# A diffusion trunk on one core: the first vectors in blocks, attention heads in pairs, the norm chain reordered, and unread matmuls in five norms' waits

## The reference

```python
def rmsnorm(x, g): return x * rsqrt(mean(x * x) + 1e-6) * g
def ffn_half(x, (shift, scale, gate), g, w_gu, w_d):
    hg, hu = split((rmsnorm(x, g) * (1 + scale) + shift) @ w_gu)      # D_FF = 2816
    return x + 0.5 * gate * ((silu(hg) * hu) @ w_d)
for l in range(2):
    xl, xc = ffn_half(xl, ...), ffn_half(xc, ...)
    hl, hc = modulated rmsnorm of each
    l == 0: conv = silu(layernorm(depthwise_conv31(val * sigmoid(gate))))
            att  = window attention, 8 heads of 64, 2 KV heads, rotary, a sink per head;
                   latents see latents within 128 and all the context, context sees context
            y = concat(conv, att) @ w_out
    l == 1: y = bidirectional chunkwise mLSTM, 4 heads of 256, output for the latents only
    x += gate * y; ffn_half again (layer 1: latents only)
return rmsnorm(xl, final_norm)
```

## Time and profile before

| | us |
|---|---|
| runs | 1919.63, 1926.95, 1926.68 (median 1926.68) |
| profiled execution | 1918.44, of which the span from first to last instruction 1916.7 |
| PE matmuls busy | 1819.4 (95%) |
| DVE / ACT busy | 869.5 (45%) / 626.4 (33%) |
| mean granted PE clock | 0.974 |

### The profile page before, as it was taken

One profiled execution on the slowest core, in us unless ns is written; L12 is line 12 of the kernel. 1 busy time (PEld: TensorE's weight loads), 2 busy tenths in 40 slices (PEclk: granted clock), 3 DMA queues, 4 the chain that ended last, 5 costly groups with the idle time before them and its releaser, 6 DMA issues.

```text
span 1916.7 us, 25184 instructions
## 1 busy us (share of the span) xinstructions
PE 1819.4 (95%) x10083; PEld 1490.1 (78%) x10083; DVE 869.5 (45%) x1335; ACT 626.4 (33%) x849; POOL 36.2 (2%) x72
## 2 busy tenths in 40 slices
PE   3999999999889999999999999999998999899996
PEld 1788888877544668888888688888886998889996
DVE  2433332345878663333233633333344436765554
ACT  2332122223445432222222432222224323544342
POOL 0000000000001000000000000000000000000000
PEclk7999999999899989999999999999998999999998
DMA  8522452243138444222323422233123212354543
GB/s 340 225 88 88 176 191 94 69 153 146 45 130 309 154 158 172 103 83 101 109 71 101 180 88 95 86 105 109 63 93 153 88 67 90 110 197 174 188 170 105
DMA packets 39107, 252.39 MB, mean 132 GB/s; under 512 B 4464, under 2 KB 5872, under 8 KB 14448
## 3 DMA queue, kind: packets, MB, share of 16 engines
q1 hardware_dynamic: 29232, 179.91, 26.5%
q0 software_dynamic: 9792, 71.31, 9.7%
HBM read 250.15 MB, written 1.05 MB: 131 GB/s over the span
## 4 chain that ended last, share of the span: by engine, by line
PE 90%; DVE 5%; ACT 2%; issue 1%; DMA 1%; SPq 0%; ACTq 0%; DVEq 0%
PE ps L432 27%; PE ps L434 27%; PE ps L433 27%; PE ps L468 3%; DVE w_lo L1176 1%; PE ps L632 1%; DMA xT<-in_xT 1%; DVE y L1359 1%; PE ps L606 1%; PE ps L745 1%; PE ps L774 1%; PE ps L492 1%; ACT w_hi L877 1%; PE ps L615 1%; DVE acc L1189 0%
## 5 line engine op out<-in xcount | busy, mean ns | idle before, releaser
L432 PE MATMUL ps<-hn_hi,w_hi 128*128 128x512 f32 (+2 forms) x1784 | 648.6, 364 | 10.2 <-DVE hn_lo L1253 8.3
L433 PE MATMUL ps<-hn_lo,w_hi 128*128 128x512 f32 (+2 forms) x1784 | 640.8, 359 | 0.0
L434 PE MATMUL ps<-hn_hi,w_lo 128*128 128x512 f32 (+2 forms) x1784 | 640.4, 359 | 0.0
L1176 DVE TENSOR_TENSOR w_lo<-raw,w_hi 128x2048 fp32r<-128x2048 f32 (+2 forms) x184 | 377.0, 2049 | 566.3 <-ACT w_hi L877 566.1
L877 ACT ACTIVATE w_hi<-raw 128x2048 fp32r<-128x2048 f32 (+2 forms) x184 | 316.6, 1721 | 777.5 <-PE ps L434 774.1
L432 PEld LDWEIGHTS ps<-hn_hi,w_hi 128*128 128x128 f32 (+1 forms) x1784 | 339.5, 190 | 74.8 <-issue 21.8
L434 PEld LDWEIGHTS ps<-hn_hi,w_lo 128*128 128x128 f32 (+1 forms) x1784 | 339.4, 190 | 50.5
L433 PEld LDWEIGHTS ps<-hn_lo,w_hi 128*128 128x128 f32 (+1 forms) x1784 | 339.8, 190 | 48.6 <-issue 0.5
L432 PE MATMUL ps<-a_hi,w_hi 128*128 128x512 f32 (+1 forms) x704 | 255.6, 363 | 1.7 <-DVE a_lo L1291 1.7
L433 PE MATMUL ps<-a_lo,w_hi 128*128 128x512 f32 (+1 forms) x704 | 255.2, 363 | 0.0
L434 PE MATMUL ps<-a_hi,w_lo 128*128 128x512 f32 (+1 forms) x704 | 255.2, 362 | 0.0
(11 more groups left out here) (189 smaller groups left out, 1162.4 us busy)
## 6 DMA issues: line engine op xcount, KB each, us to landing
raw<-in_w_up SPq DMA_DIRECT2D x88, 1024.0 KB, 4.8
mod_raw<-in_mod_w POOLq DMA_DIRECT2D x68, 1024.0 KB, 7.3
raw<-in_w_downA SPq DMA_DIRECT2D x32, 768.0 KB, 4.3
raw<-in_w_downB SPq DMA_DIRECT2D x32, 640.0 KB, 3.9
raw<-in_w_od_in SPq DMA_DIRECT2D x16, 1024.0 KB, 4.8
raw<-in_w_ev_in SPq DMA_DIRECT2D x7, 1024.0 KB, 4.8
mod_raw<-in_mod_w SPq DMA_DIRECT2D x4, 1024.0 KB, 10.1
raw<-in_w_ev_out SPq DMA_DIRECT2D x4, 1024.0 KB, 4.8
```

The lines of the kernel that those rows point to most:

```text
L432: pe.matmul(o, lh, rh, start=first, stop=False)
L433: pe.matmul(o, lh, rl, start=False, stop=False)
L434: return pe.matmul(o, ll, rh, start=False, stop=last)
L1176: dve.tensor_tensor(w_lo[:, u0 % 2, 0:n], raw[:, u0 % 2, 0:n], w_hi[:, u0 % 2, 0:n], ALU.subtract).then_inc(lo_made, 1)
```

## The change

- **Start.** x is loaded first, in four transfers. Jobs 0 and 1 are stored as eight blocks, one for each output tile k, with both vectors' columns; `block_products`, `block_columns`, `block_rows` and `block_vectors` make the two vectors of tile k just ahead of tile k's normalisation. POOL begins with job 2.
- **Norm chain.** The first square goes straight to acc and the last is not added: PE sums acc and sq[1] in two accumulating matmuls, so each norm has 6 additions instead of 8 and no clearing. The split of the second next unit (LATE_UNIT) moves from ahead of the last square and the reciprocal to behind the root on ACT and behind rstd on DVE.
- **Two units side by side.** `first_units` works the first two units after a norm tile by tile together for 5 tiles (2 tiles where there are 256 tokens), then ends the one and the other.
- **keep_busy.** In norms 1 to 5 PE does 3 matmuls on resident weights ahead of the spreading and 8 after the last quarter; their result is not read.
- **Attention.** A step now holds both heads of a pair: 16 steps. Scores of the latents use banks 4 and 5, of the context bank 1's halves; the weights are in prod or sq[0]; transposes use banks 6 and 7 both; values alternate between h2 = 0 and 1. From step 10 two quarters of a job are done per step. 30 taps stand before the loop.
- **Norm 4.** The gate unit runs three tiles ahead of the key unit; the gates' transposes are inside the key unit.

```diff
         def _(sp):
-            for q in range(4):
-                sp.dma_start(mod_raw[:, 2 * q:2 * q + 2], t["mod_w"][0][:, 2 * q:2 * q + 2]).then_inc(mod_first[q], 16)
-            sp.dma_start(xT[:], t["xT"]).then_inc(x_in, 16)
+            def block(b):
+                if b >= 4:
+                    sp.wait_ge(mod_mm, b - 3)
+                sp.dma_start(block_place(b), t["mod_first"][b]).then_inc(mod_first[b % 4], 16)
+            block(0)
             load(U["f0upA"], 0, 0, t["w_up"][0, 0], UNIT)
+            block(1)
+            load(U["f0upA"], 1, 0, t["w_up"][0, 1], UNIT)
+            for b in range(2, KT):
+                block(b)
...
         def _(pe):
+            def keep_busy(n, count):
+                u = LATE_UNIT[n] - 1
+                pe.wait_ge(lo_made, u + 1)
+                for _ in range(count):
+                    pe.matmul(ps[:, bank(u, 1), :], w_hi[:, u % 2, 0:P], w_hi[:, u % 2, 0:TOK], start=True, stop=True)
             def norm(n):
...
                 for i in range(W[n] // P):
-                    last = pe.matmul(ps[:, 6, i:i + 1], acc[:, i * P:(i + 1) * P], ones[:, 0:1], start=True, stop=True)
+                    pe.matmul(ps[:, 6, i:i + 1], acc[:, i * P:(i + 1) * P], ones[:, 0:1], start=True, stop=False)
+                    last = pe.matmul(ps[:, 6, i:i + 1], sq[:, 1, i * P:(i + 1) * P], ones[:, 0:1], start=False, stop=True)
                 last.then_inc(norm_mm, 1)
                 if job:
                     mod_products(job, 2, 3)
+                    keep_busy(n, 3)
                 pe.wait_ge(rstd_made, n + 1)
                 pe.matmul(ps[:, 7, 0:W[n]], ones, rstd[:, 0:W[n]], start=True, stop=True).then_inc(rstd_mm, 1)
                 if job:
                     mod_products(job, 3, 4)
+                    keep_busy(n, 8)
+            def first_units(u0, n, w, between=None):
+                ready = hn_ready(n)
+                order = [(j, k) for k in range(side(w)) for j in range(2)]
+                order += [(j, k) for j in range(2) for k in range(side(w), KT)]
+                for j, k in order:
+                    if j == 0:
+                        ready(k)
+                    if k == 0:
+                        begin(u0 + j)
+                    for b in range(2):
+                        o = b * KT * P + k * P
+                        last = three(ps[:, bank(u0 + j, b), 0:w], weights(u0 + j, o, o + P),
+                                     (hn_hi[:, k, 0:w], hn_lo[:, k, 0:w]), k == 0, k == KT - 1)
+                    if k == KT - 1:
+                        last.then_inc(unit_mm, 1)
+                        if j == 0 and between:
+                            between()
+                    if n == 0 and j == 0 and k + 1 < KT:
+                        block_columns(k + 1)
+                    if n == 0 and (j, k) in PRODUCTS_BEHIND:
+                        block_products(PRODUCTS_BEHIND[j, k])
...
+            def score(j, h2):
+                tt, s, qt = ATT[j]
+                if h2 == 0 and j >= 2:
+                    pe.wait_ge(exp_made, j - 1)
+                if h2 == 1 and s == 1:
+                    pe.wait_ge(s_half, j // 2 + 1)
...
+            def values(tt, s):
...
+                for i, kt in enumerate(att_keys(s)):
+                    for h2 in range(2):
+                        last = pe.matmul(ps[64 * h2:64 * h2 + 64, 0, 0:LAT], v_att[:, kt, 64 * h2:64 * h2 + 64],
+                                         turned_place(s)[:, h2, i, :], start=(i == 0), stop=(kt == 3))
...
+            BEHIND = 3
+            for step in range(KT + BEHIND):
+                if step < KT:
+                    k = step
...
+                    last = three(ps[0:16, bank(u), :], weights(u, k * 16, (k + 1) * 16),
+                                 (hn_hi[:, k, :], hn_lo[:, k, :]), k == 0, k == KT - 1)
+                if step >= BEHIND:
+                    k = step - BEHIND
+                    if k == 0:
+                        begin(u + 1)
...
         def _(act):
             def norm(n):
                 norm_root(n)
+                head_of(LATE_UNIT[n])
                 if n < 6:
                     norm_heads(n)
...
         def _(dve):
             def norm(n):
                 norm_gain(n)
                 norm_rstd(n)
+                rest_of(LATE_UNIT[n])
                 norm_apply(n)
```

More of the change, by code:

```diff
@@ L377, in ffn @@
                 for part, n in zip("AB", PARTS):
-                    if name == "f0" and part == "A":
-                        load(U["f0upA"], 1, 0, t["w_up"][f, 1], UNIT)
-                        first = 1
-                    else:
-                        first = 0
+                    first = 1 if name == "f0" and part == "A" else 0
                     with sp.Fori(first, n // 2) as r:
@@ L417, in _ @@
         def _(pool):
-            for m in range(1, JOBS):
+            for m in range(2, JOBS):
                 if m == JOBS - 1:
@@ L552, in two @@
                 return b * KT * P + k * P
-            for c in range(2):
-                unit(E + c, 0, 2, KT, TOK, (hn_hi, hn_lo), two, hn_ready(1) if c == 0 else None)
+            pe.wait_ge(mats_in, 16)
+            first_units(E, 1, TOK)
             def rotate(i):
@@ new lines, in _ @@
+            NJ = len(ATT)
+            pe.wait_ge(unit_evac, E + 5)
+            score(0, 0)
+            score(0, 1)
+            for j in range(NJ + 7):
+                between = [(conv_step, a) for a in CONV_AT.get(j, ())]
+                between += [(mod_products, (m, q, q + 1)) for m, q in att_quarters(j)]
+                if j + 1 < NJ:
+                    score(j + 1, 0)
+                    if ATT[j + 1][1] == 1:
+                        step, a = between.pop(0)
+                        step(*a)
+                    score(j + 1, 1)
+                for step, a in between:
+                    step(*a)
@@ L659, in _ @@
+                for m in att_rows(j):
+                    mod_columns(m)
             pe.wait_ge(pT_made, NJ)
@@ L1224, in norm, with norm_scaled @@
                 norm_rstd(n)
+                rest_of(LATE_UNIT[n])
                 norm_apply(n)
+            def norm_scaled(n, k):
+                if k >= 2 and n < 6:
+                    dve.wait_ge(hn_made, KT * n + k - 1)
+                for s in streams(W[n]):
+                    gain = modT[:, 3 * n + 1, k, s:s + 1] if n < 6 else col(GAIN[n][0], k)
+                    last = dve.scalar_tensor_tensor(out=t_ring[:, k % 2, tokens(s)], in0=xT[:, k, tokens(s)],
+                                                    scalar=gain, in1=ps[:, 7, tokens(s)], op0=ALU.mult, op1=ALU.mult)
+                last.then_inc(t_made if n < 6 else y_made, 1)
@@ new lines, in norm_rest, with block_vectors @@
+            def norm_rest(n, k):
+                dve.wait_ge(hn_hi_made, KT * n + k + 1)
+                for s in streams(W[n]):
+                    last = dve.scalar_tensor_tensor(out=hn_lo[:, k, tokens(s)], in0=t_ring[:, k % 2, tokens(s)],
+                                                    scalar=modT[:, 3 * n, k, s:s + 1], in1=hn_hi[:, k, tokens(s)],
+                                                    op0=ALU.add, op1=ALU.subtract)
+                last.then_inc(hn_made, 1)
+            def block_vectors(b):
+                dve.wait_ge(mod_tr, b + 1)
+                bias = cols[:, COLS["mod_b"][0]:COLS["mod_b"][0] + 2 * KT].rearrange("p (m k) -> p k m", m=2)[:, b, :]
+                dve.tensor_tensor(modT[:, 0:2, b, :], ps[:, 5, 0:4].rearrange("p (m s) -> p m s", s=2),
+                                  bias.unsqueeze(2).to_broadcast([P, 2, 2]), ALU.add).then_inc(mod_made, 1)
+                dve.wait_ge(mod_made, b + 1)
+                link(dve.tensor_scalar(modT[:, 1, b, :], modT[:, 1, b, :], 1.0, col("ffn1", b), ALU.add, ALU.mult))
```

472 lines of the change are left out of this document (251 added, 221 removed).

## The result

The changed kernel takes 1910.84 us (median of 4 runs, 1910.32 to 1915.58) against 1924.55 us for the kernel before on the same chip (4 runs): a ratio of 0.9944, interval 0.9925 to 0.9963. It is 13.7 us faster, where 31.5 were forecast; 1910.8 lies at the upper end of the range. A second set of runs of it gave 0.9925 [0.9906, 0.9945], so the gain is between 11 and 15 us (10.8 and 14.4 by the two ratios, 13.7 and 15.0 by the medians). Its profiled run took 1915.58 us, with a span of 1913.4.

What follows compares the result with a forecast made beforehand. The matmul engine, busy 95% of 1916.7 us, was taken as the bound, so only its waits, repeated work and low clock could give time. Gains 1.8 + 6.2 + 3.5 + 20 = 31.5 off 1918.4, plus 8.2: 1895 us, range 1878 to 1911.

Steps and rivals of the forecast that it cites:

- B: Rival: in attention, paired heads run one after the other on PE; 1903 us, chance 0.2.
- C: Rival: the norms' unread matmuls don't hold the clock, costing 12 us in five norms; 1907 us, chance 0.15.
- Step 5, PE's work and the pairing: Attention loop: paired heads run at once on array halves, cutting PE's work from 122 to 101 us.
- Step 5, rounds 0 to 9: Attention loop's first ten rounds: three full engines in lockstep take 50 us, bounds 43 and 58, against 54.0 before.
- Step 5, the tail: Attention loop from round 10: rounds 10 to 15 take DVE 37 us, then remaining jobs' loads 27.
- Step 1, the start: Start up to unit 2: x loaded first, unit 2 at 73.7 us; gain 1.8, bounds gain 5.5 and loss 4.5.
- Steps 2 and 3, norms 1, 2, 3, 5: Norm waits and the first two units side by side behind them: gain 6.2 us together.
- Step 4, norm 4: Norm 4 and gate unit: gate work hidden under key matmuls, 44.55 to 41.0 us; gain 3.5.
- A: The forecast itself, whole kernel: 1895 us, own range 1886 to 1903, chance 0.45.
- Outside them PE is at 1.00 clock with no gap: Outside the start, five norms and attention loop, PE never waits or slows, so those parts cost the same.
- E: Rival: the paired attention loop loses its overlap, rounds of 9.6 us run in series; 1961 us, chance 0.05.
- D: Rival: all low-clock time in the kernel is given back, PE kept full everywhere; 1875 us, chance 0.1.

Runs made afterwards that it cites:

- e6: Changed kernel with the loop's two gates by Tanh at half scale in place of Sigmoid: 1906.06 us, 0.9908; loop 127.2.
- e13: Changed kernel with a context pair's second score matmul issued right behind the first, no convolution step between: 1912.23 us, 0.9934.
- e14: Changed kernel with context-pair scores issued back to back and VectorE taking the two gated values one round later: 1908.24 us, 0.9912.
- e3: Changed kernel with the attention loop of the kernel before (32 single-head steps): 1913.41 us, 0.9949; loop 133.0.
- e12: The kernel before, unchanged, run once more for a second profile: span 1917.2 us, loop 133.0.
- e5: Changed kernel loading only half of each weight row for modulation jobs 7 to 11, every instruction kept: 1896.94 us, 0.9860; loop 117.9.
- e8: Changed kernel with two of the loop's six modulation jobs moved out, four staying: 1903.32 us, 0.9891; loop 112.4.
- e9: Changed kernel with the single-head loop of the kernel before and two of six modulation jobs moved out: 1916.49 us, 0.9983; loop 129.0.
- e4: Changed kernel with the first two units behind norms 1, 2, 3 and 5 worked one after the other: 1911.30 us, 0.9941.
- e7: Changed kernel with all eight input tiles of norm 0's first two units side by side, not five: 1904.57 us, 0.9897.
- e2: Changed kernel without the eleven unread matmuls in each of norms 1 to 5: 1918.61 us, 0.9974.
- e11: Changed kernel with eight tiles side by side, Tanh gates, four loop jobs, plus 32 unread matmuls in the loop: 1902.06 us, 0.9892.

## Why the prediction was wrong

The sign was right, the size was not: 31.5 us were forecast and 13.7 measured. It failed in one term above all, attention, forecast at 20 us (bounds 8 and 30) and worth 4. The prediction's own sign of being wrong, a loop over 125 us, came true (129.5 and 130.0). That 1910.8 still lies inside 1878 to 1911 is luck: the upper end was set by rivals B and C, and what made the loop long was neither.

- **Step 5, PE's work and the pairing: the pairing right, the sum by luck.** Both pairs run at once. PE is 100 us busy in the loop against 101 forecast, but 49.7 and 50.3 in its two parts, where 41 and 60 were forecast: 17 us of the first ran at 1.2 GHz.
- **Step 5, rounds 0 to 9: the miss.** Forecast 50 us (bounds 43 and 58), measured 62.0 and 63.2, over both bounds. DVE's and ACT's busy times were right, 41.3 (43 forecast) and 41.7 (42). The failing step is "three engines that full, in lockstep, I put at 50": a free choice between bounds. The two engines wait in turn for one another and for PE, and are two thirds busy. Table loads make some 2 us of the 12 (e6); order on PE's and VectorE's queues makes none (e13, e14); jobs' loads do not run yet (DMA share 0.05). The low clock explains little: e3 and e12 took 52.7 us each with 6 and 14.5 us at 1.2 GHz, and after 62.0 and 63.2 with 17 and 24. The rest is the chain from engine to engine, as the traces read; no run shortened it by more than these 2 us.
- **Step 5, the tail: right in kind.** 64 us were forecast for rounds 10 to the end (37 and 27), 67.5 measured, VectorE first (25.10 of 25.38 us busy), then the loads as said (e5, e8). What the prediction did not do was carry this back: five jobs are 21 MB, 52 us at the 404 GB/s of 590 to 612 us, and can't start before job 6's products. With w_ev_out's 2.1 MB, whose loads were issued at 568.9, and job 12's first quarters, the 67.5 us moved 25.2 MB, 62 us at that rate. A first part that grows from 54 to 62 us therefore moves the loads' end too, and a faster PE can't take it back. That is where most of the gain of the pairs stayed, as e9 shows. What sharing the engines with w_ev_out costs, which the prediction put at up to 5 us, no run separates; the whole tail missed by 3.5.
- **A term that was missing: 0 to 3 us behind the loop.** PE waits for loads at the end of the tail, falls to 1.2 GHz, and the next stage can begin so (0.95 in 632.16:687.99, 52.8 us before). The means of the two profiles give 2.6; in e4 and e7, whose loops have the same jobs, and in e3, e5 and e9 no low clock stands behind the loop and the stretch takes 52.9.
- **Step 1, the start: wrong in sign, within its bounds.** First matmul 24.4 (23.6 forecast), tile pitch 5.28 (5.2), tile 7 at 65.6 (64.0). The step that failed is the sum taken at the full clock: 78.16 and not 73.7 is 1.6 us in tile 7's arrival, 1.5 in its six matmuls (2.9 and not 1.4) and 1.4 in the products (5.18 and not 3.7), all of it beside a clock of 0.50. The second profile has it as 2.8, 1.4 and 0.2. e7, with PE busy on unit 1's tiles there, has the clock at 1.00 and unit 2 at 72.9, so holding three tiles back was the cause. The loss of 3.6 in the table is at its high end: over all eleven profiles with this start it is 1.5 to 4.0 against before's mean.
- **Steps 2 and 3, norms 1, 2, 3, 5: 4.6 of 6.2.** Waits of 11.02 and 9.02 us against 11.2 and 8.9, and a stall of 1.07 ahead of the third unit in norm 1 against 0.95. Norm 2's wait was 12.2 (12.4 forecast) in one profile and 13.9, 6.8 of it at 1.2 GHz, in the other, over the 13 that the prediction gave as a sign of being wrong; that is 0.8 of the 1.6 us missing in the mean. Side by side is worth 2 to 3 us.
- **Step 4, norm 4: 3.2 of 3.5.**
- **The clock in the norms.** A counted their gain inside steps 2 and 3 without a price of its own for the unread matmuls. They are the largest single part, 9.2 us in the medians, with norm 2 held in one profile of two. Rival C put their failure at 12; leaving them out (e2) cost 9.
- Rivals B, C and E are out (a round takes 6.2 us, not 9.6). Of D, "all low-clock time given back", 9 us came true in the norms and nothing in the loop, where the low-clock time grew: 35 and 40 us at 1.2 GHz in the loop after (e11's expectation has 44, which neither profile shows), 10 in e3, 20 and 17 in the two profiles of before.
- **"Outside them PE is at 1.00 clock with no gap" was a misreading, without effect on the sum.** Both kernels have some 12 us at 1.2 GHz at the very end, and stretches at it among the small matmuls between norm 4 and norm 5, where the second profile of before took 3.4 us more than the first.

Open: which stages hold the part of the median gain that single profiles don't show, and what would shorten the chain of the first ten rounds.

## What to carry to other kernels

Before pricing a faster engine in a loop, write down when its loads may start and how long they must take; if that sum ends the loop, a faster engine turns its gain into a wait, and the load is what must be moved (here to stages with the DMA engines a third busy: pairing was worth 4 us before that move and 18 after it). An engine's busy share doesn't give the time of a short loop of three engines (41, 42 and 50 us busy took 62): price it by its chain, from one engine to the next. Matmuls on data that is already loaded, put in the waits of the norms, cost nothing there and paid behind them (11.02 us with and 11.01 without, 23.6 and 25.2 behind); in a loop whose own chain passes through TensorE they only lengthened it (114.4 and not 110.1).

## What the runs showed of the hardware that was not expected

- Two 512-column fp32 score matmuls on the two row halves of the array took 1.13 us, what one took before; eight value matmuls on two column halves took 1.95, so 0.24 each where single ones took 0.5.
- The clock's fall was paid after the wait: behind one in which PE was 7.0 of 11.0 us busy the granted clock was 0.93 and 96 matmuls took 25.2 us; behind one in which it was 9.65 busy the clock stayed at 1.00 and they took 23.6.
- A single execution of either kernel scatters by 4 to 5 us about its median, more than the forecast gave the start or norm 4, while the stretch from unit 2 to norm 1 took 346.0 us in both profiles of before.
